# Preparing the first down-projection activations after the last weight splits instead of before them, at three up-to-down passages of a two-block network

## The reference

```python
# first block
h2 = rmsnorm(x, g_pre_mlp)
a = jnp.square(jax.nn.relu(jnp.einsum('bsd,df->bsf', h2, w_up)))   # 1024 -> 4096
ff = jnp.einsum('bsf,fd->bsd', a, w_down)                           # 4096 -> 1024
x = x + rmsnorm(ff, g_post_mlp)
...
# second block, each of two layers
h2 = _rmsnorm(x, g_ffn[l])
z = _dwconv(h2 @ w_up[l], w_dw_ffn[l], b_dw_ffn[l])                 # 1024 -> 2 x 2816
zg, zv = jnp.split(z, 2, axis=-1)
x = x + (jax.nn.silu(zg) * zv) @ w_down[l]                          # 2816 -> 1024
```

## Time and profile before

| | |
|---|---|
| time, 3 runs | median 2043.99 us (2041.3 to 2044.41) |
| the profiled execution | 2043.99 us |
| its span in the profile | 2042.3 us |
| busy: TensorE | 1952.7 us, 96%, 8419 matmuls |
| busy: vector engine | 1195.6 us, 59%, 1960 instructions |
| busy: scalar engine | 958.1 us, 47%, 1722 instructions |
| busy: GpSimd | 147.2 us, 7% |
| mean granted TensorE clock | 0.988 of full speed |

### The profile page before, as it was taken

The page is one execution under the profiler, slowest core; times in us unless marked ns, Lnnn a source line. Parts: engine busy times, 40 slices in busy tenths (PEclk is TensorE's granted clock), DMA queues, the critical chain, the costliest instruction groups (busy, mean ns, idle before and its releaser), DMA issues.

```text
span 2042.3 us, 25795 instructions
## 1 busy us (share of the span) xinstructions
PE 1952.7 (96%) x8419; PEld 1540.2 (75%) x8419; DVE 1195.6 (59%) x1960; ACT 958.1 (47%) x1722; POOL 147.2 (7%) x148
## 2 busy tenths in 40 slices
PE   8999989799999988999999999999999999999997
PEld 6777778578888866765678888887766578888886
DVE  4555446643343346888566666436698757656534
ACT  4655563343443333477553444334377554434432
POOL 2111000100000003220010000003120010000000
PEclk9999989899999999999999999999999999999998
DMA  4222213133332222221123333333221033333322
GB/s 136 62 64 68 70 54 104 42 94 96 98 98 94 96 78 63 62 37 37 47 83 103 98 89 106 95 96 88 67 43 42 22 95 92 92 103 93 102 94 82
DMA packets 163423, 162.44 MB, mean 80 GB/s; under 512 B 46840, under 2 KB 121550, under 8 KB 163340
## 3 DMA queue, kind: packets, MB, share of 16 engines
q1 hardware_dynamic: 163236, 161.36, 27.1%
q10 hardware_dynamic: 104, 0.03, 0.0%
HBM read 159.24 MB, written 2.10 MB: 79 GB/s over the span
## 4 chain that ended last, share of the span: by engine, by line
PE 88%; DVE 6%; ACT 3%; issue 1%; POOL 1%; DMA 0%; SPq 0%; DVEq 0%; ACTq 0%; POOLq 0%
PE bank_b L2062 15%; PE bank_b L2064 15%; PE bank_b L2063 15%; PE bank_a L2062 12%; PE bank_a L2064 12%; PE bank_a L2063 12%; PE bank_b L2353 3%; PE bank_b L2451 2%; PE bank_a L2164 1%; PE bank_a L2437 1%; DVE x_t L1338 1%; DVE arena L1341 1%; DVE w_lo L1338 1%; DVE arena L1338 1%; DVE h_lo L1341 1%
## 5 line engine op out<-in xcount | busy, mean ns | idle before, releaser
L1338 DVE TENSOR_TENSOR w_lo<-w_raw,w_hi 128x512 fp32r<-128x512 f32 (+3 forms) x621 | 428.3, 702 | 611.0 <-ACT w_hi L1053 365.4
L1053 ACT ACTIVATE w_hi<-w_raw 128x512 fp32r<-128x512 f32 (+3 forms) x396 | 233.0, 599 | 441.9 <-PE bank_b L2064 227.8
L2062 PE MATMUL bank_b<-h_hi,w_hi 128*128 128x512 f32 x944 | 371.2, 393 | 7.4 <-DVE var L1356 3.9
L2063 PE MATMUL bank_b<-h_lo,w_hi 128*128 128x512 f32 x944 | 367.9, 390 | 0.0
L2064 PE MATMUL bank_b<-h_hi,w_lo 128*128 128x512 f32 x944 | 367.8, 390 | 0.0
L2062 PE MATMUL bank_a<-h_hi,w_hi 128*128 128x512 f32 x592 | 235.2, 397 | 30.8 <-DVE h_lo L1341 16.3
L771 ACT ACTIVATE w_hi<-w_raw 128x512 fp32r<-128x512 f32 x225 | 137.8, 629 | 259.4 <-PE bank_b L2064 138.5
L1341 DVE SCALAR_TENSOR_TENSOR arena<-arena,cols_all 128x512 f32<-128x512 f32 x350 | 244.9, 750 | 0.1
L2063 PE MATMUL bank_a<-h_lo,w_hi 128*128 128x512 f32 x592 | 233.1, 394 | 0.0
L2064 PE MATMUL bank_a<-h_hi,w_lo 128*128 128x512 f32 x592 | 233.0, 394 | 0.0
L2062 PEld LDWEIGHTS bank_b<-h_hi,w_hi 128*128 128x128 f32 x944 | 177.5, 188 | 49.0 <-issue 5.0
(11 more groups left out here) (262 smaller groups left out, 2495.9 us busy)
## 6 DMA issues: line engine op xcount, KB each, us to landing
w_raw<-in_w_up_dram SPq DMA_DIRECT2D x240, 256.0 KB, 3.0
w_raw<-in_w_down_dram SPq DMA_DIRECT2D x152, 256.0 KB, 2.5
w_raw<-in_w_in_dram SPq DMA_DIRECT2D x64, 128.0 KB, 2.3
w_raw<-in_w_gate_dram SPq DMA_DIRECT2D x32, 256.0 KB, 2.9
w_raw<-in_w_in_dram SPq DMA_DIRECT2D x32, 256.0 KB, 2.6
w_raw<-in_w_o_dram SPq DMA_DIRECT2D x32, 256.0 KB, 2.6
w_raw<-in_w_out_dram SPq DMA_DIRECT2D x16, 256.0 KB, 2.6
w_raw<-in_w_in_dram SPq DMA_DIRECT2D x16, 192.0 KB, 2.3
```

Source lines behind the costliest of these rows:

```text
L1053: nc.scalar.activation(w_hi[:, s, 0:c], w_raw[:, s, 0:c], ACT.Copy).then_inc(w_round, 1)
L1338: return nc.vector.tensor_tensor(out_, a, b, op)
L2062: nc.tensor.matmul(out_, a_hi, b_hi, start=start, stop=False, skip_group_check=loose)
L2063: nc.tensor.matmul(out_, a_hi, b_lo, start=False, stop=False, skip_group_check=loose)
```

## The change

At each of the three passages (block 1, and both layers of block 2) the four `act_split` are put behind the scalar splits of the four down chunks, and the four `act_lo` behind the vector splits of the same chunks. No instruction is added or removed, and all waits keep their constants.

```diff
 # scalar engine, block 1
+            for k in range(4, KT):
+                split1(N_UP + SLOTS + (F1G - 1) * KT + k)
+
             def act_split(acts, k, first=0, i=0):
...
             for k in range(4):
                 act_split(act1, k)
-            for k in range(4, KT):
-                split1(N_UP + SLOTS + (F1G - 1) * KT + k)
             up1_out(F1G - 1)
...
 # scalar engine, block 2, each layer
                 mid_and_silu(F2G - 2)
+                for k in range(4, KT):
+                    split2(M_UP + SLOTS + (F2G - 1) * KT + k)
+
                 for k in range(4):
                     act_split(act2, k, was["a_ready"])
-                for k in range(4, KT):
-                    split2(M_UP + SLOTS + (F2G - 1) * KT + k)
                 mid_and_silu(F2G - 1)
...
 # vector engine, block 1
+            for k in range(4, KT):
+                split_lo(N_UP + SLOTS + (F1G - 1) * KT + k)
+
             def act_lo(acts, k, first=0, i=0):
...
             for k in range(4):
                 act_lo(act1, k)
-            for k in range(4, KT):
-                split_lo(N_UP + SLOTS + (F1G - 1) * KT + k)
             up1_act(F1G - 1)
...
 # vector engine, block 2, each layer
                 ffn_tiles(F2G - 2)
+                for k in range(4, KT):
+                    split2_lo(M_UP + SLOTS + (F2G - 1) * KT + k)
+
                 for k in range(4):
                     act_lo(act2, k, was["as_round"])
-                for k in range(4, KT):
-                    split2_lo(M_UP + SLOTS + (F2G - 1) * KT + k)
                 ffn_tiles(F2G - 1)
```

## The result

The changed kernel takes 2052.86 us, median of 4 runs (2052.21 to 2054.88), against 2043.82 us for the kernel before (4 runs, 2041.3 to 2044.41): 9.0 us more, ratio 1.0051 with a 95% interval of 1.0039 to 1.0062. The forecast was 2051.3 us, slower, in a range of 2048.5 to 2054.5. So the direction and the mechanism came out as said, and the size was 1.7 us low in the loss of 7.3. A second set on another occasion gave 2053.13 against 2043.1 us, 10.0 us. With these four there are 22 executions of the changed kernel in the first result, from 2050.66 to 2058.13 us with a median of 2053.13; one more, at 7913.65 us, was in a slow state and is left out everywhere.

The account below looks back on a forecast made before the run. The prediction took TensorE to bound the passages, busy 40.00 us of 40. Three times 2.44 us (2.30 wait, 0.14 restart) is 7.3 us; span 2042.3 + 7.3 = 2049.6, with 1.7 around it 2051.3 us, range 2048.5 to 2054.5.

Parts of the forecast that it names:

- gap 2.30 forecast: At each of the three passages, TensorE's first down matmul starts at 581.24 against 578.94 (block 1's times), 2.30 us late.
- restart to full pace: TensorE's matmuls behind each new wait: 0.14 us more, mostly the first weight load, no longer covered.
- The vector instruction to TensorE's restart: From the start of the first activation remainder on the vector engine to TensorE going on: 0.73 us.
- The multiplications out of bank_b: In block 2, they end near 1284.5 and TensorE wants the bank at 1285.9: margin 1.4 us, no second wait.
- What was removed: Four activation jobs ahead of the first weight split; its w_lo comes 0.24 us earlier, in block 2 at most 2.41; value nothing.
- the clock at the new gaps: Idle TensorE of 2.1 us at each passage: 0 taken for lost clock, 2.9 us a place kept for the upper end.
- the signs that it had named for being wrong: TensorE running through a passage, gaps below 1.4 us, matmuls behind them at 0.43 us pitch, or a wait on bank_b.
- rival 1: The clock falls at the new gaps: 2.9 us at one place gives 2054.2 us, all three 2060.0; 8 in 100.
- three gaps at full clock: The forecast itself: 2.44 us lost at each of the three passages, 7.3 us in all, time 2051.3 us; 82 in 100.
- the upper end: High end of the range, 2054.5 us, set by a clock fall at one place and by a second wait at bank_b.

## Why the prediction was right, and where its size was off

**The mechanism.** Shown: one tile behind one split at each place. Putting that split last, or only that tile first, takes the three gaps away, and moving the vector engine's part alone makes all three. The worked-out start times hold within 0.1 us: gap 2.30 forecast, 2.36 measured; restart to full pace 0.14 and 0.12; sum 2.44 and 2.48. The vector instruction to TensorE's restart took 0.83 us in place of the 0.73 taken from the earlier trace rows, and the remainder began 0.61 behind the w_lo, not 0.65.

**Covers.** The multiplications out of bank_b were forecast with 1.4 us to spare: in the trace after they end at 1287.94 and TensorE takes the bank at 1289.44, 1.5 us. That this margin is real and small is shown by the run with tile 0 early, where TensorE is not late and the margin is below nothing.

```profile
1285.46 2.48 DVE L1340 TENSOR_TENSOR arena<-bank_b,rstd 128x512 f32<-128x512 f32 x4
```

```profile
1289.44 0.39 PE L2066 MATMUL bank_b<-split,w_hi 128*128 128x512 f32 x1
```

**What was removed.** Worth nothing, as said: no kernel here with the earlier weight splits is faster than before.

**The clock.** This is the term that was mis-sized. The forecast took 0 for the clock at the new gaps and gave its fall a chance of 8 in 100, since a like gap of 2.79 us in the earlier trace rows had left it at 1.00. But one of the signs that it had named for being wrong is in the trace: behind the third gap the matmuls go at the 0.43 us pitch of half clock. What came is nearer to rival 1 at one place (2054.2) than to three gaps at full clock, the case given 82 in 100, and the time lies in the range because the upper end kept room for one fall.

The profiles of the changed kernel, of the vector order alone and of the one-block kernels hold 13 gaps of 2.20 us: behind 5 of them the clock fell (the third gap in both profiles of the changed kernel, the first and third with the vector order alone, block 1's in its second profile), behind 8 not. Behind the 4 gaps of 4.06 and 4.48 us it fell each time, behind the 7 passages filled with matmuls, with the change or without it, never. A fall costs 1.6 us here, less than the 2.9 taken from the earlier trace rows: there the clock was low for 5.8 us behind the restart, here for some 3.7. 5 of 13 at 1.6 us is 0.6 us a gap, 1.8 in all; measured are 2.3 +- 0.6 more in the clock's part, and 7.44 + 2.3 is 9.7 us, between the two differences of medians, 9.0 and 10.0. The Trainium skill (TensorE: Matmul & The Clock Gate, Part 1) says of the warm-up at a kernel's start that the moment of the switch to full clock differs between runs of one kernel. For the falls in mid-kernel the runs here show the like: block 2's two gaps passed at full clock in one execution, and executions of the changed kernel lie up to 7.5 us apart, with mean clocks of 0.985 to 0.989.

One row that had stayed at full clock was let decide against the other, since it looked more like the new gaps. Each was one draw: the same wait of 2.79 us near 1400 us stands in all 14 profiles kept here, and behind it the clock fell in 6 of them (1.00 in the other 8). The trace of before held two more that the forecast did not use: behind 2.71 us of idle time at 785.55 the clock stayed at full speed, and behind 2.57 us at 2026.47 it was 0.66 and then 0.50 in stretches of 2 us. So two of the four waits of 2.57 to 2.87 us had a fall behind them; neither of the two falls is between matmuls as dense as those at the passages, but they spoke for a price.

**What stays open.** Block 1's gap alone brings 2.3 us of clock loss and all three together bring the same 2.3, where by the falls counted one should bring 0.6. The profiles point at where the rest may sit. From a matmul 10 us behind block 1's passage (588.91 in the profile of before) to the last up matmul of block 2's first layer (1277.81) it is 688.90 us, with the old wait at 785 us inside and no new gap. The seven profiles with an idle gap in block 1 have 690.4 to 690.7 us there, with a fall of the clock behind that old wait each time. Of the seven without it five have 688.9 to 689.0 and no such fall; but the kernel with block 1's gap filled has 690.55 and the one with three splits ahead 690.57. So a new gap seems to make a fall some 200 us later more likely, and the fall behind 787.35 in the profile after may be the change's own; 14 single executions do not prove it, and how the falls depend on each other was not settled.

The two parts do not close either. By the means over executions the loss is 10.6 us, not 9.7: at full clock 8.3 +- 0.3 are lost where three gaps make 7.44, while block 1 alone (2.7 +- 0.3) and block 2 alone (4.9 +- 0.3) fit their gaps. Nor is it known why the kernel with tile 0 early has 24.3 us in the clock's part.

## What to carry to other kernels

Where an engine's queue is ordered by hand, ask of each item what releases it: a weight split that is handed out by TensorE's own progress must not stand ahead of anything that TensorE needs at its next step, however short it is. The order may be changed up to that item (three splits of four cost nothing that could be seen). Where a second engine waits for the first, work out its queue as well: with the scalar engine's order alone changed, the vector engine stood before its first remainder with the weight splits behind it, and the loss was 20.0 us in place of 10; with the vector engine's alone changed it was that of the whole change. A new idle gap of TensorE is to be priced as its length plus the clock that it may lose, as a mean over executions, and one row at full clock does not set that to nothing.

## What the runs showed that was not expected

- The granted clock can fall behind an idle time as short as 2.20 us between dense matmuls, in 5 of 13 cases, and a fall cost 1.6 us.
- The mean clock loss was the same 2.3 us with one new gap and with three.
- Filling a gap with matmuls that do nothing useful gave 1.8 +- 0.6 us back in block 1 (2045.99 us against 2047.74), though the operand came no earlier.
- TensorE lost 0.12 to 0.14 us at each restart beyond the wait itself.
